# Moving the gather halves and the first scatter around the second down product of a mixture-of-experts turn

## The chip, the core and the metric

The kernel runs on one core of one Trainium2 chip. Its engines work side by side, each through its own queue in order, and meet only at semaphores: TensorE (PE) multiplies into psum, VectorE (DVE) and ScalarE (ACT) do elementwise work, SyncE (SP) issues the loads. The metric is the device time of one execution in microseconds, lower is better.

## What is computed

Two model blocks in one launch, for 256 tokens of width 1024. The first is a hybrid attention mixer with a mixture of 32 experts, four per token; the second has two layers of feed-forward parts, neighbourhood attention and a short convolution. The change is in the experts alone:

```python
def moe_ffn(h, router_w, router_b, w1, b1, w2, b2):
    logits = (xt @ router_w + router_b).astype(jnp.float32)
    top_v, top_e = lax.top_k(logits, TOP_K)
    gate = jax.nn.softmax(top_v, axis=-1)
    ...
        xb = xt[rows]
        hb = xb @ w1[e] + b1[e]
        g, u = hb[:, :D_EXPERT], hb[:, D_EXPERT:]
        g = jnp.minimum(g, SWIGLU_LIMIT)
        u = jnp.clip(u, -SWIGLU_LIMIT, SWIGLU_LIMIT)
        glu = g * jax.nn.sigmoid(g * SWIGLU_ALPHA)
        return ((u + 1.0) * glu) @ w2[e] + b2[e]
    ...
    out = jnp.zeros((N, D), y.dtype).at[row_tok].add(y * row_w[:, None].astype(y.dtype))
```

## The kernel before

Experts go in pairs: 16 turns of a hardware loop on every engine, then one turn for the expert with the most tokens ("over"). Each expert takes up to 64 tokens. Its weights are 12 slots of 1 MB (four for gate, four for up, four for down), so a turn has 24 slots, numbered 0 to 23: gate0 0 to 3, up0 4 to 7, gate1 8 to 11, up1 12 to 15, down0 16 to 19, down1 20 to 23; 24 and more are the next turn's.

A slot goes this way. SyncE loads it into a ring of 8 places (L655) once TensorE has used the slot 8 before. ScalarE rounds it (`high`, L898) into one of four buffers, once TensorE has used the slot 4 before. VectorE computes what the rounding left and writes it over the slot (`low`, L2150); this is called a split here. TensorE multiplies with both parts (L1492), eight matmuls a slot, with `xg` (gathered tokens, high and low parts side by side) for gate and up, and `hid` for down.

Between the products TensorE turns the rows of a product into columns (`turn_rows`, L1507; with the gates of the selection, L1511), after ScalarE copied them out of psum (L905; the turned selection L910). VectorE adds bias and clamps in `gate_half` (L2169, L2175); ScalarE does the swish (L916); VectorE goes on in `up_half` (L2169, L2179, L2182 to L2184), whose end makes `hid`. `select` (L2126, L2127) compares token places with slot numbers for the next pair: `sel` for the gather, `selG` with gates for the scatter. TensorE gathers the next pair's tokens with `sel` in two halves (`gather`, L1465), ScalarE copies each half into `xg` (`gathered`, L884), and `result(e)` scatters the down rows of expert e back to tokens (L1529), both experts into the same two psum pairs of banks; VectorE adds these to `acc` (`add_result`, L2193).

Psum has four places of two banks. MOE_UNITS lists a turn's psum uses in the order in which TensorE fills them, MOE_PLACES the place of each; TensorE opens a use when the earlier holder of its place is freed by the engine that read it. The order of all work is written out by hand, for each engine apart, in the bodies named `experts`.

## Time and profile before

| | |
|---|---|
| runs | 3110.52, 3103.82 and 8970.65 us, median 3110.52 us |
| profiled execution | 3108.63 us, its span 3106.5 us |
| granted TensorE clock over the span | 0.931 |
| TensorE matmuls | 2827.1 us, 91% of the span |
| VectorE | 2124.6 us, 68% |
| ScalarE | 1531.3 us, 49% |
| DMA | 776.10 MB, mean 250 GB/s |
| VectorE's splits in the expert stage, 396 | 882.4 us, 2287 ns each |
| ScalarE's roundings there, 396 | 736.9 us, 1907 ns each |
| loads of expert weights | 396 of 1024.0 KB, median 8.4 us from issue to landing |

Shares are means over stages with different limits. The expert stage lies between about 545 and 1745 us of the span. Engine times are of instructions, waits not included; in timelines a bracket gives the idle time of the engine just before the row and what ended it.

### The profile page before, as it was taken

How to read it: one execution, taken by the hardware profiler on the slowest of the kernel's cores; microseconds unless marked ns; L12 is line 12 of the kernel's file. 1: busy time of each engine (PE TensorE's matmuls, PEld its weight loads, DVE VectorE, ACT ScalarE, POOL GpSimd, SP SyncE). 2: the span in 40 equal slices, each digit the busy share in tenths (PEclk: the TensorE clock that was granted, in tenths of full speed). 3: DMA queues.
4: the chain of work that ended last, by engine and by line, in shares of the span. 5: the costliest groups of instructions: out<-in, count | busy, mean ns of one | idle time of the engine just before them, and what ended most of it. 6: DMA issues, size and time to landing. Idle time of an engine off the chain costs nothing.

```text
span 3106.5 us, 43548 instructions
## 1 busy us (share of the span) xinstructions
PE 2827.1 (91%) x17548; PEld 2555.3 (82%) x17548; DVE 2124.6 (68%) x1902; ACT 1531.3 (49%) x1287; POOL 11.1 (0%) x7
## 2 busy tenths in 40 slices
PE   5998988899999999989999799999879999998998
PEld 5987877777777777777777699999868999997898
DVE  5345663899999999998899777676433664554354
ACT  0022211877777777777777444343342334432242
POOL 0000000000000000000000100000000000000000
PEclk8887886899999999999999899999989999999999
DMA  9663452788888888888888676776513774544462
GB/s 370 214 217 135 149 191 96 320 332 354 355 358 354 358 358 355 357 336 342 351 337 356 209 256 246 258 272 244 173 45 129 265 258 155 185 163 136 135 191 81
DMA packets 172402, 776.10 MB, mean 250 GB/s; under 512 B 12112, under 2 KB 37712, under 8 KB 121328
## 3 DMA queue, kind: packets, MB, share of 16 engines
q1 hardware_dynamic: 168352, 767.08, 65.6%
q10 hardware_dynamic: 3920, 7.11, 0.8%
q8 instruction: 103, 1.69, 0.2%
q14 instruction: 27, 0.22, 0.0%
HBM read 773.10 MB, written 1.05 MB: 249 GB/s over the span
## 4 chain that ended last, share of the span: by engine, by line
PE 66%; DVE 15%; issue 10%; ACT 6%; DMA 2%; DVEq 0%; ACTq 0%; SPq 0%
PE psum L1169 11%; PE psum L1171 11%; PE psum L1167 11%; PE psum L1492 8%; DVE w_low L2150 8%; PE psum L1130 7%; ACT w_high L898 4%; PE psum L1273 4%; PE psum L1529 4%; PE psum L1213 2%; DVE mod_sums L1753 2%; PE psum L1231 1%; DMA ring<-in_exp_w 1%; DVE arena L2169 1%; PE psum L1335 1%
## 5 line engine op out<-in xcount | busy, mean ns | idle before, releaser
L2150 DVE TENSOR_TENSOR w_low<-ring,w_high 128x2048 fp32r<-128x2048 f32 x396 | 882.4, 2287 | 60.6 <-ACT w_high L898 48.4
L898 ACT ACTIVATE w_high<-ring 128x2048 fp32r<-128x2048 f32 x396 | 736.9, 1907 | 133.4 <-PE psum L1492 131.3
L2283 DVE TENSOR_TENSOR w_low<-ring,w_high 128x2048 fp32r<-128x2048 f32 (+1 forms) x199 | 434.1, 2185 | 431.0 <-ACT w_high L989 429.3
L989 ACT ACTIVATE w_high<-ring 128x2048 fp32r<-128x2048 f32 (+1 forms) x199 | 363.7, 1830 | 597.0 <-PE psum L1171 507.2
L1167 PE MATMUL psum<-h_high,w_high 128*128 128x256 f32 x2144 | 611.0, 285 | 35.9 <-issue 34.0
L1169 PE MATMUL psum<-h_low,w_high 128*128 128x256 f32 x2144 | 614.4, 287 | 0.0
L1171 PE MATMUL psum<-h_high,w_low 128*128 128x256 f32 x2144 | 614.2, 286 | 0.0
L1167 PEld LDWEIGHTS psum<-h_high,w_high 128*128 128x128 f32 x2144 | 417.1, 195 | 38.3 <-issue 36.3
L1169 PEld LDWEIGHTS psum<-h_low,w_high 128*128 128x128 f32 x2144 | 411.8, 192 | 0.0
L1171 PEld LDWEIGHTS psum<-h_high,w_low 128*128 128x128 f32 x2144 | 409.4, 191 | 0.0
L1492 PE MATMUL psum<-w_high,xg 128*128 128x512 f32 x1056 | 343.1, 406 | 10.3 <-DVE w_low L2150 10.2
L1492 PE MATMUL psum<-w_low,xg 128*128 128x512 f32 x1056 | 333.5, 397 | 0.0
L1492 PE MATMUL psum<-w_high,hid 128*128 128x512 f32 x528 | 194.1, 452 | 98.5 <-DVE hid L2184 77.0
L1753 DVE SCALAR_TENSOR_TENSOR mod_sums<-ring,cs,mod_sums 128x1024 f32<-128x1024 f32 x203 | 266.3, 1326 | 4.8 <-DMA ring<-in_mod_w 0.4
L1167 PE MATMUL psum<-m_high,w_high 128*128 128x256 f32 x880 | 247.6, 281 | 0.0
L1492 PEld LDWEIGHTS psum<-w_high,xg 128*128 128x128 f32 x1056 | 193.8, 189 | 65.2 <-DVE w_low L2150 22.7
L1169 PE MATMUL psum<-m_low,w_high 128*128 128x256 f32 x880 | 247.2, 281 | 0.0
L1171 PE MATMUL psum<-m_high,w_low 128*128 128x256 f32 x880 | 247.2, 281 | 0.0
L1492 PEld LDWEIGHTS psum<-w_low,xg 128*128 128x128 f32 x1056 | 199.4, 189 | 48.7
L1492 PEld LDWEIGHTS psum<-w_high,hid 128*128 128x128 f32 x528 | 107.5, 215 | 133.3 <-issue 71.7
L1492 PE MATMUL psum<-w_low,hid 128*128 128x512 f32 x528 | 181.1, 426 | 0.0
L1167 PEld LDWEIGHTS psum<-m_high,w_high 128*128 128x128 f32 x880 | 165.8, 188 | 0.1
(260 smaller groups left out, 3393.7 us busy)
## 6 DMA issues: line engine op xcount, KB each, us to landing
ring<-in_exp_w SPq DMA_DIRECT2D x396, 1024.0 KB, 8.4
ring<-in_ffn_w SPq DMA_DIRECT2D x135, 1024.0 KB, 5.1
ring<-in_mod_w SPq DMA_DIRECT2D x96, 1024.0 KB, 5.2
ring<-in_ffn_w SPq DMA_DIRECT2D x40, 768.0 KB, 4.6
ring<-in_w_in SPq DMA_DIRECT2D x24, 1024.0 KB, 7.9
ring<-in_even_w_in SPq DMA_DIRECT2D x12, 1024.0 KB, 6.8
ring<-in_conv_w_in SPq DMA_DIRECT2D x12, 1024.0 KB, 4.9
ring<-in_w_branch SPq DMA_DIRECT2D x6, 1024.0 KB, 5.3
```

What stands on the lines that cost most here:

```text
L898: act.activation(high_ap(j, D), slot_ap(PLAN.moe_slot + j), ACT.Copy).then_inc(sem("expert_high_ready" + c.x), 1)
L989: act.activation(high_ap(m, cols), slot_ap(s, 2, cols), ACT.Copy).then_inc(sem("w_high_ready"), 1)
L1130: mm = pe.matmul(unit(u0 + j // 4)[:, (j % 4) * T:(j % 4 + 1) * T], w[:, k % 2, (c0 + j) * P:(c0 + j + 1) * P], rhs(k), start=(k == 0 and ...
L1167: pe.matmul(dst, wh[:, k % 2, cols], high[:, k, :], start=first, stop=False, skip_group_check=True)
L1169: pe.matmul(dst, wh[:, k % 2, cols], low[:, k, :], start=False, stop=False, skip_group_check=True)
L1171: mm = pe.matmul(dst, wl[:, k % 2, cols], high[:, k, :], start=False, stop=last, skip_group_check=True)
L1273: mm = pe.matmul(unit(u)[:, j * T:(j + 1) * T], w[:, k, j * P:(j + 1) * P], hT[:, k, :], start=(k == 0 and j == 0), stop=(k == DC - 1), sk ...
L1492: mm = pe.matmul(u[:, cols], x_parts(k), w[:, k % 2, cols], start=(k == 0 and w is wh), stop=(k == DC - 1 and w is wl), skip_group_check=True)
L1529: mm = pe.matmul(c.unit(name)[:, (k % 4) * T:(k % 4 + 1) * T], moe_buf(f"y_rows{e}")[:, k * P:(k + 1) * P], moe_buf(f"selT{e}"), start=(e ...
L1753: last = dve.scalar_tensor_tensor(part, w[:, k % 2, :], cond, part, ALU.mult, ALU.add)
L2150: dve.tensor_tensor(low_ap(PLAN.moe_slot + j, D), slot_ap(PLAN.moe_slot + j), high_ap(j, D).bitcast(F32), ALU.subtract).then_inc(sem("expe ...
L2283: dve.tensor_tensor(low_ap(s, cols), slot_ap(s, 2, cols), high_ap(m, cols).bitcast(F32), ALU.subtract).then_inc(sem("w_split"), 1)
```

## The change

It reorders the work of a turn on TensorE, VectorE and ScalarE and rewrites `select`; what is computed stays.

- TensorE: first gather half, scatter of expert 0, down1, second gather half, scatter of expert 1. Before: both gather halves, down1, both scatters. The psum places are dealt out anew.
- VectorE: slot 19 is split after the second gate half instead of before, the selection stands behind it, and the second up half comes before slots 20 and 21. The next turn's slot 3 (27) is split in this turn. In the over turn slots 8 to 10 are split before the gate half.
- ScalarE: slot 20 is rounded before the second swish, the first gather half copied before slot 23 is rounded, the second one behind the down1 rows, and slot 27 rounded at this turn's end.
- `select`: six two-tensor operations (two compares over both experts, then four products with the gates) with one wait between instead of eight tensor-scalar ones.

```diff
-             "gather0", "gather1", "down1", "result", "resultb")
-MOE_PLACES = (0, 1, 2, 3, 0, 1, 2, 3, 0, 1, 2, 3, 2, 1)
+             "gather0", "down1", "gather1", "result", "resultb")
+MOE_PLACES = (0, 1, 2, 3, 2, 1, 0, 2, 3, 1, 1, 0, 3, 2)
...
-NEXT_SLOTS = (TURN_SLOTS, TURN_SLOTS + 1, TURN_SLOTS + 2)
+NEXT_SLOTS = tuple(range(TURN_SLOTS, TURN_SLOTS + HIGHS))
...
                 high(c, 19)
                 selection_turned(1)
+                high(c, 20)
                 swish(1)
-                high(c, 20, 21, 22)
+                high(c, 21, 22)
                 rows("down0", "y_rows0", 1.0 / ALPHA)
+                c.await_unit(act, "gather0")
+                gathered(0, c.unit("gather0"), c.x)
                 high(c, 23)
-                for half in range(2):
-                    c.await_unit(act, f"gather{half}")
-                    gathered(half, c.unit(f"gather{half}"), c.x)
                 if not last:
-                    high(c, *NEXT_SLOTS)
+                    high(c, *NEXT_SLOTS[:-1])
                 rows("down1", "y_rows1", 1.0 / ALPHA)
-
-            high(first_turn(0), 0, 1, 2)
+                c.await_unit(act, "gather1")
+                gathered(1, c.unit("gather1"), c.x)
+                if not last:
+                    high(c, *NEXT_SLOTS[-1:])
+
+            high(first_turn(0), 0, 1, 2, 3)
...
                 down(0, range(DC // 2, DC), 16)
-                gather_next()
+                gather_next(0)
+                result(0, False)
+                gather_taken(0)
                 down(1, range(DC), 20)
-                gathers_taken()
-                result(0, False)
+                gather_next(1)
                 result(1, True)
+                gather_taken(1)
...
-            def select(col, x):
-
-                for e in range(2):
-                    for b in range(TB):
-                        p_, g_ = col(512 + COLS_E * b + e), col(580 + COLS_E * b + e)
-                        dve.tensor_scalar(sel[:, b, e, :], slot_no, p_, None, ALU.is_equal)
-                        last = dve.tensor_scalar(selG[:, b, e, :, :], slot_no[:, None, :].broadcast_to([P, 2, CAP]),
-                                                 p_, g_, ALU.is_equal, ALU.mult)
+            def select(pair_of, x, done):
+
+                slots = slot_no[:, None, :].broadcast_to([P, 2, CAP])
+                for b in range(TB):
+                    of = pair_of(512 + COLS_E * b)[:, :, None].broadcast_to([P, 2, CAP])
+                    last = dve.tensor_tensor(sel[:, b, :, :], slots, of, ALU.is_equal)
+                done(last)
+                for b in range(TB):
+                    of = pair_of(580 + COLS_E * b)[:, :, None].broadcast_to([P, 2, CAP])
+                    for d in range(2):
+                        last = dve.tensor_tensor(selG[:, b, :, d, :], sel[:, b, :, :].bitcast(F32), of, ALU.mult)
                 last.then_inc(sem("sel_ready" + x), 1)
...
                 if over:
-                    low(c, 3, 4, 5, 6, 7)
+                    low(c, 4, 5, 6, 7, 8, 9, 10)
                     gate_half(0)
-                    low(c, 8, 9)
                     up_half(0)
-                    low(c, 10, 11)
+                    low(c, 11)
...
-                low(c, 16, 17, 18, 19)
+                low(c, 16, 17, 18)
                 gate_half(1)
-
-                select(lambda at: small[:, bass.ds(c.columns + (at + 2), 1)], c.x)
-                low(c, 20, 21)
+                low(c, 19)
+
+                select(lambda at: small[:, bass.ds(c.columns + (at + 2), 2)], c.x, steps.link)
                 up_half(1)
-                low(c, 22, 23)
+                low(c, 20, 21, 22, 23)
                 if not last:
                     low(c, *NEXT_SLOTS)
                 add_result()
```

What stands on VectorE between the second gate half (L2175 before, L2181 after) and the next splits (w_low<-ring,w_high). Before, from the end of the gate half; the twelve rows left out are the last four three times more:

```order
L2175 TENSOR_SCALAR arena<-arena 128x512 [waits psum_free2]
L2126 ISA
L2126 TENSOR_SCALAR sel<-consts,small 128x64
L2127 ISA
L2127 TENSOR_SCALAR arena<-consts,small 128x128
...
L2150 TENSOR_TENSOR w_low<-ring,w_high 128x2048 [waits expert_high_ready]
L2149 REGISTER_ALU
L2150 TENSOR_TENSOR w_low<-ring,w_high 128x2048 [waits expert_high_ready]
L601 REGISTER_ALU
L2169 ISA [waits psum_full]
L2169 TENSOR_TENSOR arena<-psum,vecs 128x512
```

After:

```order
L2181 TENSOR_SCALAR arena<-arena 128x512 [waits psum_free0]
L2155 REGISTER_ALU
L2156 TENSOR_TENSOR w_low<-ring,w_high 128x2048 [waits expert_high_ready]
L2129 ISA
L2129 TENSOR_TENSOR sel<-consts,small 128x128
L2129 ISA
L2129 TENSOR_TENSOR sel<-consts,small 128x128
L367 REGISTER_ALU
L2134 ISA [waits dve_steps]
L2134 TENSOR_TENSOR arena<-sel,small 128x2x64 x2
...
L2175 TENSOR_TENSOR arena<-psum,vecs 128x512
```

One split (slot 19) has moved in behind the gate half, two (20 and 21) have left the stretch before the up half (L2169 before, L2175 after), and the selection has six operations with a wait.

The head of ScalarE's loop, whose first operation carries the load of an activation table. Before, it rounds slot 3, after waiting for the last psum use of the earlier turn's down1:

```order
L957 ISA
L624 ISA [waits psum_full]
L898 ACT_TABLE_LOAD
L898 ACTIVATE w_high<-ring 128x2048 [waits slot_landed3]
L618 ISA
```

After, it rounds slot 4, after waiting for TensorE to use slot 0:

```order
L960 ISA
L624 ISA [waits slots_used]
L898 ACT_TABLE_LOAD
L898 ACTIVATE w_high<-ring 128x2048 [waits slot_landed4]
L618 REGISTER_ALU
```

The rounding of slot 3 has moved to the end of the loop, and the table load stands behind another wait.

The end of ScalarE's loop, from the copy of the down1 rows (L905) on. After the change:

```order
L905 ACTIVATE arena<-psum 128x1024 [waits psum_full]
L601 REGISTER_ALU
L884 ACTIVATE xg<-psum 128x1024 [waits psum_full]
L898 ACTIVATE w_high<-ring 128x2048 [waits slot_landed3,psum_full]
L960 REGISTER_ALU
L960 COMPARE_AND_BRANCH
```

Before, the loop ended with the copy; the second gather half and slot 27 now follow it.

## Rows read from the trace of the kernel before

**Rows 1.** Timeline of ScalarE: start and duration in us; gather copies, turns 1 and 16.

```profile
604.61 1.93 ACT L884 ACTIVATE xg<-psum 128x1024 fp32r<-128x1024 f32 x2
...
1680.36 1.92 ACT L884 ACTIVATE xg<-psum 128x1024 fp32r<-128x1024 f32 x2
```

**Rows 2.** Busy time by stretch, fifteen turns; last: clock, DMA share, GB/s.

```profile
604.60:1680.30 1075.70, 987.60 (x4860) 817.26 (x4860) 978.85 (x721) 837.95 (x571) 0.00 (x0) 0.95 0.87 351
```

**Rows 3.** Timeline of TensorE, from one turn's down products into the next turn.

```profile
1018.95 0.73 PE L1492 MATMUL psum<-w_high,hid 128*128 128x512 f32 x2 [1.27 <-DVE w_low L2150]
...
1028.64 0.33 PE L1465 MATMUL psum<-sel,h_nat_high 128*128 128x128 f32 x2
...
1031.93 0.39 PE L1465 MATMUL psum<-sel,h_nat_low 128*128 128x128 f32 x2
...
1036.67 1.22 PE L1492 MATMUL psum<-w_high,hid 128*128 128x512 f32 x2 [4.35 <-DVE hid L2184]
...
1046.19 7.07 PE L1529 MATMUL psum<-arena 128*128 128x256 f32 x32
...
1052.90 0.81 PE L1492 MATMUL psum<-w_high,xg 128*128 128x512 f32 x2
...
1068.14 1.89 PE L1507 MATMUL psum<-consts,arena 128*128 128x64 f32 x16
```

**Rows 4.** Timeline of VectorE, the same turn.

```profile
1016.60 8.90 DVE L2150 TENSOR_TENSOR w_low<-ring,w_high 128x2048 fp32r<-128x2048 f32 x4
1025.42 0.68 DVE L2169 TENSOR_TENSOR arena<-psum,vecs 128x512 f32<-128x512 f32 x1
...
1026.48 0.25 DVE L2126 TENSOR_SCALAR sel<-consts,small 128x64 fp32r<-128x64 f32 x1
1026.64 0.34 DVE L2127 TENSOR_SCALAR arena<-consts,small 128x128 f32<-128x128 f32 x1
1026.90 0.25 DVE L2126 TENSOR_SCALAR sel<-consts,small 128x64 fp32r<-128x64 f32 x1
...
1029.07 4.49 DVE L2150 TENSOR_TENSOR w_low<-ring,w_high 128x2048 fp32r<-128x2048 f32 x2 [0.83 <-ACT w_high L898]
1033.48 0.68 DVE L2169 TENSOR_TENSOR arena<-psum,vecs 128x512 f32<-128x512 f32 x1
...
1042.51 6.70 DVE L2150 TENSOR_TENSOR w_low<-ring,w_high 128x2048 fp32r<-128x2048 f32 x3 [1.35 <-ACT w_high L898]
1051.57 1.23 DVE L2193 TENSOR_TENSOR arena<-psum,arena 128x1024 f32<-128x1024 f32 x1 [2.36 <-PE psum L1529]
1053.29 1.23 DVE L2193 TENSOR_TENSOR arena<-psum,arena 128x1024 f32<-128x1024 f32 x1 [0.50 <-PE psum L1529]
1055.01 6.70 DVE L2150 TENSOR_TENSOR w_low<-ring,w_high 128x2048 fp32r<-128x2048 f32 x3 [0.49 <-DVE arena L2193]
```

**Rows 5.** Timeline of ScalarE, the same turn.

```profile
1026.60 0.63 ACT L916 ACTIVATE arena<-arena 128x512 f32<-128x512 f32 x1 [6.86 <-DVE arena L2175]
...
1032.54 1.00 ACT L905 ACTIVATE arena<-psum 128x1024 f32<-128x1024 f32 x1
...
1046.38 1.02 ACT L905 ACTIVATE arena<-psum 128x1024 f32<-128x1024 f32 x1
1047.43 1.28 ACT L898 ACT_TABLE_LOAD   x1
...
1055.16 5.65 ACT L898 ACTIVATE w_high<-ring 128x2048 fp32r<-128x2048 f32 x3 [4.53 <-PE psum L1492]
```

**Rows 6.** Timelines of VectorE and of TensorE in the over turn.

```profile
1719.43 0.69 DVE L2169 TENSOR_TENSOR arena<-psum,vecs 128x512 f32<-128x512 f32 x1 [4.92 <-ACT arena L910]
...
1728.02 1.22 PE L1492 MATMUL psum<-w_high,hid 128*128 128x512 f32 x2 [7.43 <-DVE hid L2184]
```

**Rows 7.** Busy time by stretch: loads at full rate; behind the next turn's gap.

```profile
1082.00:1085.00 3.00, 3.00 (x15) 2.40 (x14) 3.00 (x2) 3.00 (x3) 0.00 (x0) 1.00 1.02 426
...
1109.00:1112.00 3.00, 3.00 (x9) 2.32 (x8) 3.00 (x2) 0.00 (x0) 0.00 (x0) 0.50 0.00 0
```

More of the change, by code:

```diff
@@ L919, in experts @@
                 if over:
-                    high(c, 3, 4, 5, 6)
+                    high(c, 4, 5, 6)
                     rows("gate0", "gate_rows")
-                    high(c, 7, 8)
+                    high(c, 7, 8, 9, 10)
                     rows("up0", "up_rows")
                     selection_turned(0)
-                    high(c, 9)
                     swish(0)
-                    high(c, 10, 11)
+                    high(c, 11)
                     rows("down0", "y_rows0", 1.0 / ALPHA)
                     return
-                high(c, 3, 4, 5, 6)
+                high(c, 4, 5, 6)
                 rows("gate0", "gate_rows")
@@ L966, in before_pairs @@
                         gathered(half, psum[:, 2 + half, :], "_x")
-                    high(x_turn(r, 0), 0, 1, 2)
+                    high(x_turn(r, 0), 0, 1, 2, 3)
                 rounds_loop(act, before_pairs, experts)
@@ L1533, in result, with gather_next, gather_taken @@
                             mm.then_inc(c.full, 1)
-                def gather_next():
+                def gather_next(half):
                     pe.wait_ge(sem("sel_ready" + c.x), c.gathers + 2)
-                    for half in range(2):
-                        c.open_unit(pe, f"gather{half}")
-                        gather(c.unit(f"gather{half}"), half).then_inc(c.full, 1)
-                def gathers_taken():
-                    pe.wait_ge(sem("xg_ready" + c.x), c.gathers * 2 + 4)
-                    for half in range(2):
-                        pe.sem_inc(c.free[MOE_PLACES[MU[f"gather{half}"]]], 1)
+                    c.open_unit(pe, f"gather{half}")
+                    gather(c.unit(f"gather{half}"), half).then_inc(c.full, 1)
+                def gather_taken(half):
+                    pe.wait_ge(sem("xg_ready" + c.x), c.gathers * 2 + (half + 3))
+                    pe.sem_inc(c.free[MOE_PLACES[MU[f"gather{half}"]]], 1)
                 pe.wait_ge(sem("xg_ready" + c.x), c.gathers * 2 + 2)
@@ L2119, in _, with first_pair @@
             slot_no = const("iota")[:, 0:CAP]
-            def select(col, x):
-                for e in range(2):
-                    for b in range(TB):
-                        p_, g_ = col(512 + COLS_E * b + e), col(580 + COLS_E * b + e)
-                        dve.tensor_scalar(sel[:, b, e, :], slot_no, p_, None, ALU.is_equal)
-                        last = dve.tensor_scalar(selG[:, b, e, :, :], slot_no[:, None, :].broadcast_to([P, 2, CAP]),
-                                                 p_, g_, ALU.is_equal, ALU.mult)
+            def select(pair_of, x, done):
[8 more added lines that the diff above has]
+                        last = dve.tensor_tensor(selG[:, b, :, d, :], sel[:, b, :, :].bitcast(F32), of, ALU.mult)
                 last.then_inc(sem("sel_ready" + x), 1)
-            def first_col(at):
-                return small[:, at:at + 1]
-            select(first_col, "")
+            def first_pair(at):
+                return small[:, at:at + 2]
+            select(first_pair, "", link)
             find_busiest()
@@ L2208, in experts @@
                 if over:
-                    low(c, 3, 4, 5, 6, 7)
+                    low(c, 4, 5, 6, 7, 8, 9, 10)
                     gate_half(0)
-                    low(c, 8, 9)
                     up_half(0)
-                    low(c, 10, 11)
+                    low(c, 11)
                     add_over()
                     return
-                low(c, 3, 4, 5, 6, 7, 8, 9, 10)
+                low(c, 4, 5, 6, 7, 8, 9, 10)
                 gate_half(0)
@@ L2230, in experts @@
                 add_result()
-            low(first_turn(0), 0, 1, 2)
+            low(first_turn(0), 0, 1, 2, 3)
             most = many(dve)
             with dve.Fori(0, PAIRS) as i:
-                steps.enter(i, 6)
+                steps.enter(i, 7)
                 experts(first_turn(i), steps)
@@ L2256, in before_pairs, with first_sel @@
                 def before_pairs(r):
+                    def first_sel(last):
+                        last.then_inc(sem("first_selected_x"), 1)
+                        dve.wait_ge(sem("first_selected_x"), r + 1)
                     dve.tensor_scalar(place2[:, :, 0:E], place2[:, :, 0:E], -float(CAP), None, ALU.add).then_inc(
@@ L2260, in before_pairs @@
                     dve.wait_ge(sem("round_shifted"), r + 1)
-                    select(first_col, "_x")
-                    low(x_turn(r, 0), 0, 1, 2)
+                    select(first_pair, "_x", first_sel)
+                    low(x_turn(r, 0), 0, 1, 2, 3)
                 def later(c, last=False):
                     steps_x.n = 0
-                    steps_x.enter(c.turn, 6)
+                    steps_x.enter(c.turn, 7)
                     experts(c, steps_x, last)
```

## The prediction

> **What bounds the kernel now.** I first looked for a regular stage. ScalarE copies the gathered tokens at 604.61 us in the first turn and at 1680.36 us in the sixteenth [rows 1]: fifteen turns in 1075.75 us, 71.7 us each, so the expert loop holds 16 x 71.7 = 1147 us of the span of 3106.5 us. Over just these turns the table of busy time by stretch [rows 2] gives TensorE 987.6 us, VectorE 978.9 us and ScalarE 838.0 us of 1075.7, and the DMA engines a share of 0.87. VectorE works 65.3 us per turn, TensorE 65.8 us, and nobody is full, so the 71.7 us come from waits that these two impose on each other.
>
> The order of one turn shows where. TensorE [rows 3] finishes the gather for the next turn (from 1028.64 to 1032.32), stands 4.35 us for the hidden activations of the second expert, runs the second down product from 1036.67 to 1046.19, 9.5 us for four slots, and then both scatters, 6.7 us, until the next turn opens at 1052.90. Four slots otherwise take 7.6 us (eight from 1052.90 to 1068.14 take 15.24). The missing 1.9 us are the clock: the first two matmuls behind the gap last 1.22 us, where the first two of a turn last 0.81, and at the same place of the next turn the granted clock is 0.50 [rows 7], the 1.2 GHz level.
>
> VectorE [rows 4] is late with these activations because two weight splits stand ahead of them (1029.07 to 1033.48), themselves after 0.83 us of waiting for ScalarE. Later it waits 1.35 us for a rounded slot, 2.36 us and 0.50 us for the scatters. ScalarE [rows 5] had idled 6.86 us before the swish, with nothing queued that it could do.
>
> DMA is not the bound: with all engines busy it moves 426 GB/s [rows 7], so a slot of 1.05 MB costs 2.5 us and 24 slots 59 us, below every turn considered here.
>
> **What the parts cost, on the traced turn.** VectorE's unit is a split: 2.2 us from start to start (8.90 us for four less 4.49 for two, halved), 2.3 us until it is ready. Its other terms are the gate half 1.06 us (1025.42 to 1026.48), the up half 3.18 us (1033.48 to 1036.67), and the selection, now four pairs started 0.16 and 0.26 us apart, 1.7 us [rows 3, 4]. An up half or split ends for VectorE where the next thing starts, at 1036.67.
>
> The new selection is six two-tensor operations of 128 elements and one wait between them. No row has that shape. From below, six starts at 0.16 us are 1.0 us; from above, six at the full 0.34 us of the dearer old one and 0.1 us for the wait are 2.1 us. I take 1.5 us: a split of 2048 elements starts 2.2 us apart, 1.08 ns per element with everything in, and 0.16 us for 64 elements leaves some 0.1 us fixed, so 0.23 us each, and 0.1 us for the wait. That is 0.2 us won, with bounds of 0.7 us won and 0.4 us lost.
>
> A rule speaks against even that. The Trainium skill (VectorE: DVE Perf Modes, section on the side-by-side cycle counts) gives an operation about 158 fixed cycles beside its elements, and its section "The DRAIN you can't avoid" lets none start before the last has left the pipe. By these, as an estimate, six operations are 1.8 us and the selection wins nothing; the total below would be 5 us later. The rows show starts 0.16 us apart behind operations that last 0.25 us, so here the next does start earlier, and the rows decide.
>
> Now the new order, from the third group of splits at 1016.60 us, where the sequence first differs. VectorE: three splits to 1023.2; gate half to 1024.3; the fourth split to 1026.5; selection to 1028.0; up half to 1031.2, against 1036.67. Splits 20 to 23 then start from 1031.2 and are ready at 1033.5, 1035.7, 1037.9 and 1040.1; 24 to 26 end at 1046.6. The gate half can come earlier since ScalarE's last work before its idle 6.86 us, done at 1019.7, is the copy of the turned selection it waits for [rows 5]; the same idle time covers the rounding of slot 20 that now stands before the swish.
>
> TensorE: the first down product ends at 1028.6 as before, the first gather half at 1030.4 (1.8 us). ScalarE copies the down rows by 1029.8, so the first scatter runs 1030.4 to 1033.8 (half of 6.7 us). Its wait on that gather's copy is covered: ScalarE has done it by 1031.6. Slot 20 is split at 1033.5, so nothing is left of the 4.35 us, nor of the slow clock. Slots 20 to 23 at 1.9 us, the last two held by their splits, end at 1042.0; gather 1.8 and scatter 3.4 end at 1047.2, against 1052.90: 5.7 us earlier.
>
> Not all of it stays. ScalarE, after 1042.0, copies rows (start 0.2 later, 1.0 us), then the second gather half (1044.0 to 1045.0) and only then rounds slot 27, to 1046.9. VectorE was free at 1046.6; it splits to 1049.1 and adds the results, 3.0 us with the loop's turn (1.23, 1.23 and 0.49 us), to 1052.1. And at the head of ScalarE's loop the table load of 1.28 us [rows 5] now stands behind the wait for slot 0 instead of in front of a slot already free (the second listing under the change). The old head starts 2.26 us after the turn's opening (1055.16 against 1052.90); now 2.26 + 1.3 + 1.9 = 5.5 us pass, and split 4 starts at 1047.2 + 5.5 = 1052.7. Before, it started one split after 1055.01, at 1057.2. Saved: **4.5 us a turn**. From here on all engines have the old sequence until the next 1016.60. Bounds for the table load are 0 (hidden) and 1.5 us (plus its issue); I take 0.6 us of it as exposed on VectorE, as it comes out above.
>
> Psum places: the rows of the first up product, turned, now use place 2, freed by the gate half at about 21 us of the turn, while TensorE wants it at 24.7 (15.2, 1.9 for the turned gate rows, 7.6); the last result half wants place 2 at about 1032.1, freed at 1028.7. Both are covered by over 3 us.
>
> The single turn for the busiest expert: its down product waited 7.43 us [rows 6], while VectorE idled 4.92 us and then, by the code, does two splits (4.4 us) between gate and up half. These move into the idle time: 3.5 us won, bounds 0 and 4.4. The first turn's head changes by nothing that I can see, since three or four splits run in one series there.
>
> **Sum.** 16 x 4.5 + 3.5 = 75.5 us off the profiled execution's 3108.6 us: 3033 us. The median shown is 1.9 us above that execution, so I predict 3035 us. About 2% (62 us, under 3048 us) is what a measurement of this kernel can tell from no change.
>
> **Rivals.**
> - *Half of it.* The second down product still runs at the low clock. All after it is then 1.9 us later: 16 x 2.6 + 3.5 = 45 us won, 3065 us. For it: VectorE's splits now hold TensorE at almost every slot of the down products. Against: the traced turn has a 1.27 us wait before slot 16 without a slow matmul.
> - *The change doesn't close the gap.* If ScalarE copied the down rows 4 us later than I have it, TensorE would stand before the scatter instead of before the product: about 3100 us. My margin there is 0.6 us, but in the trace the copy starts late (1032.54) only because three roundings precede it; one of them has moved ahead of the swish.
> - *More.* Selection at 1.0 us, the table load hidden, and the tail without loss: 4.5 + 0.5 + 0.6 + 0.3 = 5.9 us a turn, 3012 us.
> - *Slower.* TensorE's clock falls at the chain of short waits, from slot 16 on. Eight slots at twice 1.9 us cost 15 us, of which splits at 2.2 us cover 2.4; the turn is then about 12.8 us longer than mine, 8 us over the old one: 3240 us. It decides from about four slow slots: they alone cost 6.4 us and eat my gain. The old trace has slots at just this pace (16 and 17) at full speed.
>
> The Trainium skill (TensorE: Matmul & The Clock Gate, section "A second HAM failure mode") describes a swing between both clocks in a kernel whose TensorE idles briefly and often, which would be this rival. No row of this loop shows it.
>
> **Chances.** Forecast (3018 to 3050 us) 0.60, half 0.17, gap not closed 0.10, more 0.07, slower 0.06. Faster than 3048 us: most of the forecast (0.57) and "more", with a little of "half", 0.66; within 2%: 0.28; slower 0.06. The range 3012 to 3074 us leaves out "gap not closed", "slower" and a sliver of "more", under 2 in 10.
>
> **What would show it.** Turns of 67.2 us between ScalarE's copies; the wait of 4.35 us gone and no matmul pair over 0.8 us in the second down product; a VectorE without waits of 2.36 and 1.35 us, with one of 0.5 us behind the loop's turn; VectorE's share above 0.95 and the largest of all in the loop; ScalarE's table load behind its wait. A turn above 69 us, or a TensorE wait of over 2 us before the first scatter, would make the prediction wrong.

## The result

The changed kernel takes 3037.03 us as the median of four runs (3027.31 to 3043.87), the kernel before, on the same chip, 3113.11. One of the four runs before took 8970.65 us; the ratio leaves it out. It is 0.976, with a 95% interval of 0.974 to 0.979: **faster**, by 2.4%. I had predicted 3035 us. The profiled execution took 3036.2 us (span 3034.4), 72.4 us less than the profiled one of before (3108.6); my sum had said 75.5.

The expert stage of the new kernel over fifteen turns, from the start of the last VectorE operation on the first expert's hidden activations in the first turn to the same operation in the sixteenth. Columns as in [rows 2]: stretch, length, busy time of TensorE, its weight loads, VectorE, ScalarE and GpSimd with their numbers of operations, then granted clock, DMA share and GB/s:

```profile
580.66:1589.10 1008.44, 979.54 (x4863) 792.45 (x4861) 970.26 (x690) 839.45 (x571) 0.00 (x0) 0.99 0.93 374
```

That is 67.23 us a turn, where [rows 2] has 71.7. TensorE and VectorE are busy for nearly the same time as before (979.5 and 970.3 us, against 987.6 and 978.9), so it is mostly waiting that went. Both are now at 0.97 and 0.96 of the stretch, and by these shares one can't tell which of them is the bound; the experiments below say where each of them is.

TensorE in the stretch of a turn that I had worked out (here of the eighth turn; the rows of before are of the seventh), from the first slot of a down product that waits for its split (start, duration, operation, number, and in brackets the idle time before it). It answers to [rows 3]:

```profile
1054.50 0.73 PE L1495 MATMUL psum<-w_high,hid 128*128 128x512 f32 x2 [1.25 <-DVE w_low L2156]
...
1064.18 0.34 PE L1468 MATMUL psum<-sel,h_nat_high 128*128 128x128 f32 x2
...
1065.91 3.67 PE L1532 MATMUL psum<-arena 128*128 128x256 f32 x16
1069.23 0.82 PE L1495 MATMUL psum<-w_high,hid 128*128 128x512 f32 x2
...
1077.58 0.34 PE L1468 MATMUL psum<-sel,h_nat_high 128*128 128x128 f32 x2
...
1079.32 3.67 PE L1532 MATMUL psum<-arena 128*128 128x256 f32 x16
```

One gather half and one scatter now stand on each side of the second down product. It opens at 1069.23 without a wait, its first two matmuls last 0.82 us instead of the 1.22 of [rows 3], and it takes 8.35 us (to 1077.58) where it took 9.5.

VectorE in the same turn, which answers to [rows 4]:

```profile
1052.15 6.69 DVE L2156 TENSOR_TENSOR w_low<-ring,w_high 128x2048 fp32r<-128x2048 f32 x3
...
1059.83 2.29 DVE L2156 TENSOR_TENSOR w_low<-ring,w_high 128x2048 fp32r<-128x2048 f32 x1
1062.03 0.49 DVE L2129 TENSOR_TENSOR sel<-consts,small 128x128 fp32r<-128x128 f32 x2
1062.66 0.90 DVE L2134 TENSOR_TENSOR arena<-sel,small 128x128 f32<-128x128 f32 x4
1063.47 0.68 DVE L2175 TENSOR_TENSOR arena<-psum,vecs 128x512 f32<-128x512 f32 x1
...
1066.65 15.50 DVE L2156 TENSOR_TENSOR w_low<-ring,w_high 128x2048 fp32r<-128x2048 f32 x7
1082.37 2.29 DVE L2156 TENSOR_TENSOR w_low<-ring,w_high 128x2048 fp32r<-128x2048 f32 x1 [0.21 <-ACT w_high L898]
1084.58 2.56 DVE L2199 TENSOR_TENSOR arena<-psum,arena 128x1024 f32<-128x1024 f32 x2
1088.18 2.29 DVE L2156 TENSOR_TENSOR w_low<-ring,w_high 128x2048 fp32r<-128x2048 f32 x1 [1.04 <-ACT w_high L898]
```

The waits of 0.83, 1.35, 2.36 and 0.50 us of [rows 4] are gone. What is left are 0.21 us before the split of slot 27, 1.04 us before that of slot 4, and 0.31 us before that of slot 12, and each of them is for a rounding of ScalarE.

ScalarE at the end of that turn and the head of the next, which answers to [rows 5]:

```profile
1079.51 1.02 ACT L884 ACTIVATE xg<-psum 128x1024 fp32r<-128x1024 f32 x1 [0.71 <-PE psum L1468]
1080.43 1.90 ACT L898 ACTIVATE w_high<-ring 128x2048 fp32r<-128x2048 f32 x1
1084.94 1.28 ACT L898 ACT_TABLE_LOAD   x1 [2.60 <-PE psum L1495]
1086.23 5.52 ACT L898 ACTIVATE w_high<-ring 128x2048 fp32r<-128x2048 f32 x3
```

The copy of the second gather half ends at 1080.53 and slot 27 is rounded at 1082.33, so VectorE waits for it by a little. Then ScalarE idles 2.60 us for one of its four buffers, until TensorE has used slot 0, and only behind this wait does the table load run; this is what VectorE's 1.04 us are made of.

In the over turn TensorE's wait before its down product went from the 7.43 us of [rows 6] to this:

```profile
1648.81 1.22 PE L1495 MATMUL psum<-w_high,hid 128*128 128x512 f32 x2 [4.84 <-DVE hid L2190]
```

VectorE's first splits in the over turn, before the change and after it:

```profile
1703.41 11.10 DVE L2150 TENSOR_TENSOR w_low<-ring,w_high 128x2048 fp32r<-128x2048 f32 x5 [0.70 <-DVE mod_sums L2242]
1629.21 15.51 DVE L2156 TENSOR_TENSOR w_low<-ring,w_high 128x2048 fp32r<-128x2048 f32 x7 [0.70 <-ACT w_high L898]
```

The five are slots 3 to 7, the seven are slots 4 to 10, since slot 3 is now split a turn earlier. Slot 4, the landmark of the sum, is therefore the second of the five, split at 1705.62, and the first of the seven, split at 1629.21. From there to TensorE's scatter (1739.56 and 1659.99) are 33.94 us before and 30.78 now, 3.16 us less. From the scatter to the first reciprocal of VectorE behind it the new kernel is slower, in code that the change leaves alone (busy time by stretch, before and after):

```profile
1739.56:1756.89 17.33, 12.26 (x48) 9.73 (x48) 10.87 (x15) 7.63 (x9) 0.00 (x0) 0.90 0.31 113
1659.99:1679.26 19.27, 13.80 (x48) 10.66 (x48) 10.87 (x16) 7.63 (x9) 0.00 (x0) 0.82 0.27 101
```

That is 1.94 us more, at a granted clock of 0.82 where it was 0.90.

### The profile page after: what moved, and what is told of

It is laid out like the page before. It is cut to its first block, busy times and chain, and to the rows that moved or that the text cites. A ratio compares the mean times of both kernels' runs of the same rounds, so it can differ in the third digit from the quotient of the medians.

```text
span 3034.4 us, 43530 instructions
## 1 busy us (share of the span) xinstructions
PE 2820.3 (93%) x17548; PEld 2527.3 (83%) x17548; DVE 2114.7 (70%) x1868; ACT 1532.7 (51%) x1287; POOL 10.8 (0%) x7
## 3 DMA queue, kind: packets, MB, share of 16 engines
HBM read 773.10 MB, written 1.05 MB: 255 GB/s over the span
## 4 chain that ended last, share of the span: by engine, by line
PE 64%; DVE 19%; issue 12%; ACT 4%; DMA 1%; DVEq 0%; PEld 0%; ACTq 0%; SPq 0%; PEldq 0%
PE psum L1172 12%; PE psum L1174 12%; PE psum L1170 12%; DVE w_low L2156 11%; PE psum L1133 7%; PE psum L1495 5%; PE psum L1276 4%; PE psum L1532 2%; ACT w_high L898 2%; PE psum L1216 2%; DVE mod_sums L1756 2%; PE psum L1234 2%; PE psum L1468 1%; DVE arena L2175 1%; PE psum L1338 1%
## 5 line engine op out<-in xcount | busy, mean ns | idle before, releaser
L1495 PE MATMUL psum<-w_high,hid 128*128 128x512 f32 x528 | 181.3, 425 | 27.2 <-DVE w_low L2156 20.0
L1495 PE MATMUL psum<-w_low,hid 128*128 128x512 f32 x528 | 171.0, 406 | 0.0
L1172 PEld LDWEIGHTS psum<-m_low,w_high 128*128 128x128 f32 x880 | 165.8, 188 | 0.1
```

The source lines that it names most:

```text
L1172: pe.matmul(dst, wh[:, k % 2, cols], low[:, k, :], start=False, stop=False, skip_group_check=True)
L1495: mm = pe.matmul(u[:, cols], x_parts(k), w[:, k % 2, cols], start=(k == 0 and w is wh), stop=(k == DC - 1 and w is wl), skip_group_check=True)
```

## The experiments

All are edits of the changed kernel. Four questions: which half of the reordering earns the 4.5 us a turn; what the selection and the table load cost; which engine bounds the turn now; and why some turns are 0.5 us longer. A "turn" below is the distance of one turn's last operation on the second expert's hidden activations from the next turn's; for the changed kernel it is 67.10 us in most turns and 67.23 in the mean. Times given with a range are medians of several runs, the others come from one execution, and there the length of a turn is what counts.

### TensorE's new order, with VectorE's and ScalarE's old one

The order around the second up half is put back. The new selection, the early copy of the first gather half and the new places of slot 27 stay.

```diff
 ScalarE
-high(c, 20)
 swish(1)
-high(c, 21, 22)
+high(c, 20, 21, 22)
 VectorE
-low(c, 16, 17, 18)
+low(c, 16, 17, 18, 19)
 gate_half(1)
-low(c, 19)
 ... selection ...
+low(c, 20, 21)
 up_half(1)
-low(c, 20, 21, 22, 23)
+low(c, 22, 23)
```

> The changed kernel with VectorE's and ScalarE's order around the second up half put back (splits 16 to 19 before the gate half, 20 and 21 before the up half, the rounding of slot 20 behind the swish); TensorE keeps the new order. Theory (the gain needs the hidden activations early AND the scatter in front of the second down product): TensorE waits about 3.2 us before the first scatter, since the down rows are copied late, split 4 comes 2.5 us later than in the changed kernel, a turn of about 69.6 us, the whole 16 x 2.5 = 40 us slower than the changed kernel (about 3077). Rival (TensorE's order alone makes the gain): a turn within 0.5 us of the changed kernel's 67.1. Rival (VectorE's order alone): a turn of 71 us or more.

Measured: 3102.57 us (3090.85 to 3108.95), ratio to the kernel before 0.997 (0.996 to 0.999), turns of 71.43 us and now and then 72.18, 71.63 in the mean. Nearly the whole gain is gone. TensorE's timeline, behind the first gather half and then behind the second:

```profile
1026.46 5.38 PE L1531 MATMUL psum<-arena 128*128 128x256 f32 x16 [3.14 <-ACT arena L905]
...
1040.87 3.67 PE L1531 MATMUL psum<-arena 128*128 128x256 f32 x16
```

and VectorE's over the same time:

```profile
1035.76 6.70 DVE L2155 TENSOR_TENSOR w_low<-ring,w_high 128x2048 fp32r<-128x2048 f32 x3 [1.82 <-ACT w_high L898]
1043.92 2.29 DVE L2155 TENSOR_TENSOR w_low<-ring,w_high 128x2048 fp32r<-128x2048 f32 x1 [1.47 <-ACT w_high L898]
```

The wait moved where I expected it, in front of the first scatter, and by 3.14 us had the size I expected (3.2). I had the turn 2 us too short (69.6), and the rows show most of it: behind that wait the scatter takes 5.38 us instead of 3.67, the clock at its lower level again. So the kernel gets next to nothing from TensorE's order unless the copy of the down rows comes early. By the order of the code that is what moving the rounding of slot 20 ahead of the swish and the gate half ahead of split 19 does; which of the two does it was not run apart.

### The new order on VectorE and ScalarE, with both gather halves ahead of the second down product and both scatters behind it

```diff
-"gather0", "down1", "gather1", "result", "resultb"
+"gather0", "gather1", "down1", "result", "resultb"
 TensorE
 gather_next(0)
-result(0, False)
+gather_next(1)
 gather_taken(0)
 down(1, range(DC), 20)
-gather_next(1)
+result(0, False)
 result(1, True)
```

> The changed kernel with TensorE's order put back: both gather halves before, both scatters behind the second down product; VectorE and ScalarE keep the new orders. Theory (both parts count): the second down product starts as early as in the changed kernel, but 3.4 us of scatter stand behind it instead of 1.8 us of gather, so the next turn opens and split 4 comes about 1.5 us later: a turn of 68.6 us, 16 x 1.5 = 24 us slower than the changed kernel (about 3061). Rival (TensorE's order alone makes the gain): a turn of 71 us. Rival (VectorE's order alone): 67.1 us, no difference to the changed kernel.

Measured: 3063.01 us (3052.43 to 3067.73), ratio 0.985 (0.983 to 0.987), turns of 68.77 us, 68.88 in the mean; expected 68.6 and 3061. TensorE, then VectorE at the head of the next turn:

```profile
1019.64 7.07 PE L1532 MATMUL psum<-arena 128*128 128x256 f32 x32
```

```profile
1031.92 15.50 DVE L2156 TENSOR_TENSOR w_low<-ring,w_high 128x2048 fp32r<-128x2048 f32 x7 [3.54 <-ACT w_high L898]
```

Everything but TensorE's order (early hidden activations, and with them the new selection, of which more below) is worth 71.7 less 68.9, 2.8 us a turn. Both scatters in one piece at the end then keep VectorE waiting for the head of the next turn. This turn is one of three in which it waits 3.54 us, behind a fall of the clock; in the other twelve it is 3.02 us, and in the changed kernel 1.04. The last 1.7 us of the gain need the first scatter moved forward. The two halves are not a sum: without early hidden activations the rest of the change gives 0.1 us, and on top of them TensorE's order gives 1.7.

### The old selection in the new order

```diff
 def select(...)
-    two-tensor operations of 128 elements, both experts in one: 2 + 4
+    for e in range(2): for b in range(TB): tensor_scalar is_equal; tensor_scalar is_equal, mult
```

> The changed kernel with the old selection of eight tensor-scalar operations in the new place. Theory by the rows (starts 0.16 and 0.26 us apart, 1.68 us in all, against 1.44 us now): every turn 0.24 us longer, 67.3 us, 4 us in all, too little for the total to show; the turn in the trace decides. By the fixed costs that the Trainium skill gives (VectorE: DVE Perf Modes) old and new would cost the same and the turn would stay at 67.1.

Measured: 3040.03 us in one execution, with turns of 67.34 us where the changed kernel has 67.10. The new selection, 1.44 us in the fence above (1062.03 to 1063.47), is therefore worth 0.24 us a turn, which is what the rows of both kernels give (1.68 less 1.44). By the Trainium skill's fixed cost for each operation (VectorE: DVE Perf Modes, side-by-side cycle counts and "The DRAIN you can't avoid") the eight old operations take 2.1 us, as an estimate, and the six new ones 1.8. The trace does not agree with either, since the new ones with a dependence between them fit into 1.44 us, and the old ones start 0.16 and 0.26 us apart; the second section itself lets an operation that is not held start earlier. But my expectation was wrong that by these costs the two would be alike: they put the old ones 0.3 us higher, so the 0.24 us a turn don't decide between the rows and the Trainium skill. The lengths do.

### The table load ahead of the wait

A one-element Silu at the head of ScalarE's turn, before it waits for one of its buffers:

```diff
+act.activation(stats[:, 0, 0, 0:1], stats[:, 0, 0, 0:1], ACT.Silu)
 high(c, 4, 5, 6)
```

> The changed kernel with one activation (Silu) on a single unused column at the head of ScalarE's loop, in front of the wait for slot 0. Theory (the table load behind that wait holds up split 4 and VectorE bounds the loop): the load moves in front of the wait, VectorE's 1.04 us of idle before split 4 shrink to the 0.5 us of the loop's own turn, a turn of 66.5 us, 16 x 0.55 = 9 us faster than the changed kernel (about 3028). Rival (TensorE bounds the loop, VectorE's idle costs nothing): 67.1 us a turn, no difference.

Measured: 3025.46 us (3024.11 to 3028.09), ratio 0.9725 (0.971 to 0.974), turns of 66.56 us; expected 66.5 and 3028. ScalarE's timeline shows the load moved into its idle time:

```profile
1082.47 1.28 ACT L930 ACT_TABLE_LOAD   x1
1083.76 0.20 ACT L930 ACTIVATE stats<-stats 128x1 f32<-128x1 f32 x1
1085.07 5.58 ACT L898 ACTIVATE w_high<-ring 128x2048 fp32r<-128x2048 f32 x3 [1.10 <-PE psum L1496]
```

The load costs the changed kernel 0.54 us a turn (67.10 less 66.56). I had put down 0.6. The second load of a turn, ahead of the first swish, went away too (15 loads in fifteen turns instead of 30), as the roundings run under the table that the Silu has loaded. It had cost VectorE nothing: its wait before slot 4 shrank from 1.04 to 0.49 us, and its 0.30 us before slot 12, behind the swish, stayed.

### More work for TensorE early in the turn

The first gate rows are turned twice, 1.7 us of additional TensorE work; the second pass repeats the first, and the output is the same.

```diff
-turn_rows("gate0_turn", "gate0", "gate_rows", 0)
+turn_rows("gate0_turn", "gate0", "gate_rows", 0, 1 if over else 2)
```

> The changed kernel with the eight matmuls that turn the first gate rows issued twice in each pair's turn (the same result written again): 1.7 us more work for TensorE per turn. Theory (VectorE bounds the loop, TensorE waits for it): the 1.7 us are taken from TensorE's waits, the turn stays at 67.1 us, total unchanged within 3 us of the changed kernel. Rival (TensorE, 97% busy in the loop, bounds it): 68.8 us a turn, 27 us slower.

Measured: 3068.01 us, turns of 68.85 us: all of the 1.7 us came through, against my theory that VectorE bounds the turn and TensorE has slack wherever it waits. ScalarE and then VectorE show the way it took:

```profile
1046.97 0.38 ACT L910 ACTIVATE arena<-psum 128x256 f32<-128x256 f32 x1 [2.27 <-PE psum L1514]
1047.25 1.91 ACT L898 ACTIVATE w_high<-ring 128x2048 fp32r<-128x2048 f32 x1
1049.17 1.28 ACT L916 ACT_TABLE_LOAD   x1
1050.47 0.63 ACT L916 ACTIVATE arena<-arena 128x512 f32<-128x512 f32 x1
```

```profile
1049.19 2.29 DVE L2156 TENSOR_TENSOR w_low<-ring,w_high 128x2048 fp32r<-128x2048 f32 x1 [0.42 <-ACT w_high L898]
1052.94 8.90 DVE L2156 TENSOR_TENSOR w_low<-ring,w_high 128x2048 fp32r<-128x2048 f32 x4 [1.46 <-ACT w_high L898]
```

ScalarE waits 2.27 us (0.49 in the changed kernel) for the turned selection that TensorE now makes later, and stands in front of the rounding of slot 11 with it. Behind that come the table load and the swish before slot 12. VectorE pays 0.42 and 1.46 us, where it paid 0.31 before the split of slot 12.

### More work for VectorE

Two additional two-tensor operations of 512 elements behind the selection, whose result nobody reads:

```diff
 select(...)
+for _ in range(2):
+    steps.link(dve.tensor_tensor(ub, gb, gb, ALU.add))
```

> The changed kernel with two more additions of 512 elements into the scratch of the up half, behind the selection: 1.44 us more work for VectorE per turn. Theory (VectorE bounds the loop): all of it shows, 68.5 us a turn, 16 x 1.44 = 23 us slower than the changed kernel. Rival (TensorE bounds it, VectorE has 2 us of idle a turn): at most 0.5 us a turn.

Measured: 3052.89 us, turns of 68.73 us, 1.63 more than 67.10. VectorE's timeline, the two operations and the up half behind them:

```profile
1073.30 1.41 DVE L2232 TENSOR_TENSOR arena<-arena 128x512 f32<-128x512 f32 x2
1074.94 0.69 DVE L2175 TENSOR_TENSOR arena<-psum,vecs 128x512 f32<-128x512 f32 x1 [0.23 <-DVE arena L2232]
```

From the start of the first to the up half are 1.64 us, so at this place VectorE's work comes through in full. I had put the two at 1.44 us.

### More work for TensorE where it waits

The same doubling, for the second gate rows, ahead of the wait of 1.25 us before slot 16:

```diff
-turn_rows("gate1_turn", "gate1", "gate_rows", 1)
+turn_rows("gate1_turn", "gate1", "gate_rows", 1, 2)
```

> The changed kernel with the eight matmuls that turn the second gate rows issued twice, right ahead of TensorE's 1.25 us wait before slot 16, behind which the granted clock was at its lower level in 5 of 16 turns (these are 0.5 us longer, 67.6). Theory (that wait lets the clock fall): the wait is filled, no slow matmul in the loop, every turn 67.1 us. Rival (the clock falls because of what is run there, turned rows of 64 columns, not because of the wait): slow matmuls in as many or more turns, some turns of 67.6 us or longer.

Measured: 3036.58 us, and every turn between 67.08 and 67.11 us. TensorE's timeline:

```profile
1055.71 3.68 PE L1510 MATMUL psum<-consts,arena 128*128 128x64 f32 x32
```

Here the same 1.7 us cost nothing. What is more, they made the long turns disappear. (The total doesn't show it: in this execution the code ahead of the expert stage took 5.6 us longer.) In the changed kernel five of sixteen turns hold a few slow matmuls behind the 1.25 us wait before slot 16, as this one (TensorE's timeline) does:

```profile
718.00 0.73 PE L1495 MATMUL psum<-w_high,hid 128*128 128x512 f32 x2 [1.25 <-DVE w_low L2156]
...
719.38 1.05 PE L1495 MATMUL psum<-w_high,hid 128*128 128x512 f32 x2
...
722.91 0.63 PE L1495 MATMUL psum<-w_low,hid 128*128 128x512 f32 x2
```

A pair lasts 1.05 us there and 0.63 us a little later, so the clock was at 1.2 GHz for some 3 us and then at 2.4 again. Over a stretch of 67.10 us with such matmuls the granted clock is 0.97, over the next one without them 1.00 (busy time by stretch, columns as above):

```profile
714.86:781.96 67.10, 65.33 (x322) 53.50 (x322) 64.23 (x45) 55.37 (x39) 0.00 (x0) 0.97 0.93 370
781.96:849.06 67.10, 65.16 (x325) 52.46 (x325) 64.68 (x46) 56.00 (x39) 0.00 (x0) 1.00 0.93 375
```

The turn with the slow matmuls is 67.61 us long; four of the fifteen distances are 67.6 and eleven 67.1, and the fifth slow place lies behind the last of them. I counted such places in every trace of this study. With the new order and a wait of 1.25 to 1.3 us before slot 16 there were 5, 4, 2, 4, 5 and 4 of 16 behind it (changed kernel, old selection, early table load, more TensorE work early, scatters late, more VectorE work). With the scatters late there were three more behind a second wait, of 1.13 us before slot 20. In the kernel before there were none behind its wait of 1.27 us, and none behind the 1.25 us of the first experiment; in these two the clock falls in every turn elsewhere, at the waits of 4.35 and 3.14 us. With the wait filled or shortened to 0.86 us or less (this run and the three below) there were none in 64 turns. So taking the wait away is enough; what decides in a given turn whether the clock falls behind it I can't say. Nor is the price fixed: 0.5 us in the changed kernel, 0.3 with the old selection, and nothing with more VectorE work, where all turns are 68.73 to 68.75 us.

### Three moves on ScalarE

The early table load; the rounding of slot 12 ahead of the first swish; the rounding of slot 27 ahead of the copy of the second gather half:

```diff
+act.activation(stats[:, 0, 0, 0:1], stats[:, 0, 0, 0:1], ACT.Silu)
 high(c, 4, 5, 6)
 ...
+high(c, 12)
 swish(0)
-high(c, 12, 13, 14)
+high(c, 13, 14)
 ...
+if not last: high(c, *NEXT_SLOTS[-1:])
 c.await_unit(act, "gather1")
 gathered(1, c.unit("gather1"), c.x)
-if not last: high(c, *NEXT_SLOTS[-1:])
```

> The changed kernel with three edits on ScalarE alone: the Silu activation on one unused column at the loop's head (as in early_table), slot 12 rounded before the first swish instead of behind it, and slot 27 rounded before the second gather half is copied. Theory (each idle stretch of VectorE is worth itself): early_table's turn of 66.55 us loses the 0.31 us before split 12 and the 0.20 us before split 27, with the pipe's drain of 0.08 us each, 65.9 us a turn, 10 us faster than early_table (about 3015). Rival (the last idle time of VectorE is covered by TensorE or loads): 66.5 us a turn, about 3025.

Measured: 3012.31 us (3008.07 to 3016.56), ratio 0.968 (0.9665 to 0.970), turns of 65.86 us; expected 65.9 and 3015. VectorE's timeline over a part of a turn:

```profile
1008.52 2.56 DVE L2201 TENSOR_TENSOR arena<-psum,arena 128x1024 f32<-128x1024 f32 x2
1011.57 15.50 DVE L2158 TENSOR_TENSOR w_low<-ring,w_high 128x2048 fp32r<-128x2048 f32 x7 [0.49 <-ACT w_high L898]
...
1028.05 11.10 DVE L2158 TENSOR_TENSOR w_low<-ring,w_high 128x2048 fp32r<-128x2048 f32 x5
```

One wait of 0.49 us is left in a turn. The three moves were worth 1.24 us, and the three waits that they removed summed to 0.21, 0.31 and 0.55: 1.07 us.

### The extra TensorE work early in the turn again, with the roundings ahead

The three moves, the first gate rows turned twice, and the rounding of slot 11 ahead of the copy of the turned selection:

```diff
+high(c, 11)
 selection_turned(0)
-high(c, 11)
 high(c, 12)
```

> act_three (65.86 us a turn) with the first gate rows turned twice as in pe_more, and slot 11 rounded before ScalarE copies the turned selection. pe_more lost 1.75 us a turn, with VectorE idle 0.42 us before split 11 and 1.46 us before split 12. Theory (the loss was ScalarE's order: roundings 11 and 12 stood behind the copy of the selection and the swish, which the longer turning delays): with both roundings ahead the 1.7 us of TensorE work disappear in its waits, at most 66.1 us a turn. Rival (TensorE has no room left in the first half of the turn, whatever ScalarE does): 67.5 us a turn.

Measured: 3023.91 us in one execution, turns of 66.10 us, 0.24 more than without the extra work. So it was not the work: the same 1.7 us cost 1.75 us when the roundings of slots 11 and 12 stand behind the copy that waits for them, and 0.24 when they stand in front. This run also has the early table load, so it is ScalarE's order as a whole that it clears, not one rounding.

### Work taken off VectorE

The three moves, and the rounding of the hidden activations (0.43 us on VectorE, twice a turn) done by ScalarE, while VectorE does the split that came next:

```diff
 VectorE, in up_half(e)
-steps.link(dve.tensor_scalar(hid[e][:, :, 0, :], ub, 1.0, None, ALU.mult))
+low(c, (11 if over else 16) if e == 0 else 20)
+dve.wait_ge(sem("hid_rounded" + c.x), c.turn * 2 + (e + 1))
 ScalarE
+act.wait_ge(sem("up_done" + c.x), c.turn * 2 + (e + 1))
+act.activation(hid[e][:, :, 0, :], moe_buf("up", DC), ACT.Copy)
```

> act_three with the rounding of the hidden activations (two operations of 0.43 us per turn on VectorE) moved to ScalarE, and one split (16, 20) placed on VectorE while ScalarE rounds. Theory (VectorE bounds the loop all the way round): 0.46 us from start to start twice, less a few hundredths for the new waits, comes off each turn: 65.0 us, 16 x 0.85 = 14 us faster than act_three (about 2999). Rival (the hidden activations come later to TensorE, behind a split more, and TensorE then bounds): 65.9 us or longer.

Measured: 3000.22 us (2995.24 to 3006.23), ratio 0.964 (0.962 to 0.966), turns of 64.70 us. It is the fastest of this study, 1.2% under the changed kernel. Taking away 0.86 us of VectorE's work a turn gave 1.16, more than the work itself; the rest may be the gaps of a dependent operation, which the split now fills, but I did not separate it. Busy time over fifteen turns, for the three moves alone and with the relief:

```profile
580.37:1568.24 987.87, 967.59 (x4862) 789.21 (x4861) 967.54 (x690) 826.52 (x571) 0.00 (x0) 1.00 0.95 382
```

```profile
586.01:1556.60 970.59, 961.18 (x4863) 791.53 (x4862) 952.29 (x662) 839.86 (x601) 0.00 (x0) 1.00 0.96 389
```

TensorE is at 0.99 of the second stretch and its waits for splits are down to 0.2 us. That suggests that the next gain would have to come from TensorE itself; no run here shows it.

## Why the prediction was right

**The gap.** Each landmark of the new turn came where the sum put it. Counted from the start of split 16 (1052.15), the hidden activations were ready after 14.5 us (14.6 predicted), the first gather opened after 12.0 and the first scatter after 13.8 us (12.0 and 13.8), the next turn after 30.5 (30.6), and its split 4 started after 36.03 us (36.1). TensorE's 4.35 us wait and the slow matmuls behind it are gone, and no wait stands before the first scatter. The runs with one half each show that the mechanism is the one named: without the early hidden activations the wait returns as 3.14 us elsewhere and takes 4.4 us a turn back.

**The selection.** 1.44 us against my 1.5; its worth 0.24 us a turn against 0.2. The trace went by the rows for the length of both. Setting the Trainium skill's estimate of 1.8 us for the new selection (VectorE: DVE Perf Modes, side-by-side cycle counts) against the measured 1.7 of the old one, as I did, mixed two scales: by the same costs the old one is 2.1 us.

**The table load.** I took 0.6 us of its 1.28 as exposed; taking it away gave 0.54. The small waits are there as predicted: 0.21 us before slot 27, for which the sum had 0.2 to 0.3, and 1.04 before slot 4, for which it had 0.49 and 0.6.

**The over turn.** 3.16 us up to its scatter, against 3.5. Behind the scatter 1.94 us of it are lost again (below).

**Where the sum is off.** From the head of the stage to its end the new kernel is 72.7 us shorter (1250.08 to 1177.38 us, from one reciprocal of VectorE ahead of the stage to the first behind it), against 75.5. With the split of slot 4 as the landmark, as in the sum, the parts are:

| | sum | measured |
|---|---|---|
| sixteen turns | 72.0 | 71.48 |
| over turn, to its scatter | 3.5 | 3.16 |
| from there to the end of the stage | 0 | -1.94 |

The sixteen turns are near for reasons that partly cancel. Without the slow matmuls fifteen distances between turns give 4.62 us each, a little more than my 4.5, and the end of the sixteenth turn gives 5.1; that is 2.4 us more than the sum. TensorE's clock takes 2.5: five turns with slow matmuls behind the wait before slot 16, 0.5 us each. This was my rival "Slower" in a mild form, and the sentence against it ("the traced turn has a 1.27 us wait before slot 16 without a slow matmul") was true of all sixteen turns of before and didn't carry over to the new order. The first turn's head takes 0.44 us. "The first turn's head changes by nothing that I can see" is a step that failed: the table load stands behind the wait for a buffer also in the first turn, and VectorE waits for it:

```profile
550.41 11.10 DVE L2156 TENSOR_TENSOR w_low<-ring,w_high 128x2048 fp32r<-128x2048 f32 x5 [0.59 <-ACT w_high L898]
```

The 1.9 us behind the over turn's scatter are the clock again, in code that the sum took as unchanged.

**What was luck.** Outside the stage the two profiled executions differ by 4.9 us in the code ahead of it, the new one being earlier, and by 5.5 us the other way behind it. The change doesn't touch that code, and over the twelve traces of this study the part ahead takes from 500.4 to 507.5 us. Behind the stage 10.6 us are lost in one stretch, the second block's neighbourhood attention, and 5.1 won in the rest. That stretch before and after (busy time by stretch):

```profile
2284.74:2365.25 80.51, 69.09 (x368) 55.90 (x366) 19.27 (x45) 23.35 (x43) 0.00 (x0) 0.90 0.16 53
2204.34:2295.46 91.12, 79.70 (x368) 62.48 (x366) 19.25 (x45) 22.79 (x43) 0.00 (x0) 0.78 0.14 47
```

The granted clock is 0.78 instead of 0.90. Over the twelve traces the stretch takes from 80.5 us at 0.90 to 93.5 at 0.75; why it differs between kernels with the same code there stays open. Each of these differences is larger than every term of the sum but the gap, and that they leave only 0.6 us together is chance. So is part of the nearness of 3037 to 3035: the four runs of the changed kernel, with granted clocks of 0.941 to 0.948, spread over 16.6 us, the longest with the lowest clock and the shortest with the highest. That the turn came out at 67.1 us is not.

**The rivals.** "Half of it" and "the change doesn't close the gap" are out by the timeline; the run with the old order on VectorE and ScalarE shows what the second would have looked like (3103 us; I had given it about 3100). "More" did not happen, yet two of its conditions could be brought about: with the table load hidden, slot 27 in time and slot 12 too, the kernel takes 3012 us.

**What I had wrong of the bound.** I had written that VectorE would be the largest share in the loop. It is not (0.96 against TensorE's 0.97), though it bounds the turn where I tried it: 1.64 us of additional VectorE work ahead of the second up half make the turn 1.63 us longer, and 0.86 us taken off its two up halves make it 1.16 shorter. At other places of VectorE's turn I did not try. What I would have concluded from this, that TensorE's work is free, holds before slot 16 (0.00 of 1.7 us) and not before slot 11 (1.75 of 1.7). The chain there is TensorE's turned selection, ScalarE's copy of it, ScalarE's rounding behind that copy, VectorE's split.

## What to carry to other kernels

Walk each engine's queue through one period with measured start-to-start distances, and give each wait that you remove its successor: here that gave a turn to 0.1 us. An in-order engine that serves two others, as ScalarE does here, makes its waits theirs; put what the bounding engine wants next (the roundings) ahead of what may wait (a copy, a table load), and load a table by a tiny operation ahead of a wait rather than behind it. Busy shares of 0.97 and 0.96 don't say who bounds a loop; adding the same small work at two places says where it is bound. And compare a total only after taking it apart: here code that the change leaves alone moved by up to 10.6 us with the granted clock.

## What the runs showed of the hardware

- TensorE's clock fell to 1.2 GHz behind waits of 1.25 us, in 5 of 16 turns of the same code, for some 3 us and at a cost of 0.5 us of the turn, and in none where the wait was filled with 1.7 us of matmuls. With the scatters late it also fell behind a wait of 1.13 us, in 3 of 16 turns. Behind 3.14 us of waiting sixteen scatter matmuls took 5.38 us instead of 3.67. The Trainium skill (TensorE: Matmul & The Clock Gate, section "A second HAM failure mode") describes a swing between the two clocks from brief idling between groups of matmuls; the trace shows falls of the clock of this kind here, now and then and for a short time, not as a lasting state.
- ScalarE's table load took 1.28 us, the activation began 0.01 us behind it, and the load ran behind the wait of the operation that needs it, though the engine had been idle for 2.60 us.
- Two-tensor operations of 128 elements on VectorE: two busy for 0.49 us together, four for 0.90 us. A group of six, with one dependence between them, took 1.44 us from start to the next operation's start; eight tensor-scalar ones of 64 and 128 elements in turn took 1.68 us, with the old selection.
